# A two-layer decoder step on one core: four changed orders, the last rows by products with diagonals, and 32 gate pages on SP's queue

## What is computed

```python
for i in range(2):
    mk, mv = memory tokens @ w_mem_kv[i]
    # layer 0: indexer-selected sparse attention, layer 1: forgetting attention
    q, k, v, ... = h @ w_in
    so = attend(q, [cache, k], [cache, v])          # layer 1 adds cumulative log-forget bias:
    #   lf_all = concat([pool_lf[page_table], logf_new]); c = cumsum(lf_all)
    mo = mem_attend(qm, mk, mv)
    h = layer_norm(alpha * h + concat(so, mo) @ w_o, ln1_g, ln1_b)
    h = layer_norm(alpha * h + hier_moe(h), ln2_g, ln2_b)   # top-1 of 4 groups, top-2 of 4 experts
return h (prompt rows, sample rows), keys, values, gates
```

## Time and profile before

| | |
|---|---|
| median of 3 runs | 2313.71 us (2310.28 to 2316.61) |
| profiled execution | 2314.92 us, its span 2313.1 us |
| TensorE busy | 2181.2 us, 94% of the span |
| VectorE, ScalarE busy | 669.1 us (29%), 494.5 us (21%) |
| mean granted TensorE clock | 0.973 |
| memory traffic | 647.30 MB, 280 GB/s over the span |

### The profile page before, as it was taken

How to read it: one execution, slowest core, us unless ns; L and a number is a source line. 1 busy time by engine, 2 the same in 40 slices (tenths; PEclk the granted TensorE clock), 3 DMA queues, 4 the chain that set the end, 5 groups by cost and what they waited for, 6 DMA issues and landing times.

```text
span 2313.1 us, 32005 instructions
## 1 busy us (share of the span) xinstructions
PE 2181.2 (94%) x12445; PEld 1369.2 (59%) x12445; DVE 669.1 (29%) x1226; ACT 494.5 (21%) x1115; POOL 4.3 (0%) x10
## 2 busy tenths in 40 slices
PE   8999999989999999999799999999999999998996
PEld 7778875678744344343478886545787343434433
DVE  0249941601652222212400010023017512222224
ACT  1221026400421001011300206633004210100114
POOL 0000000000000000000000000000000000000000
PEclk9999999989899999999899999989898999999998
DMA  9733658784269999999754457998542799999992
GB/s 265 224 146 110 215 159 260 236 291 146 74 262 427 391 429 402 429 392 428 291 170 136 181 174 265 359 323 303 182 146 74 311 416 395 429 393 428 387 426 120
DMA packets 209036, 647.30 MB, mean 280 GB/s; under 512 B 54840, under 2 KB 88393, under 8 KB 183305
## 3 DMA queue, kind: packets, MB, share of 16 engines
q1 hardware_dynamic: 175841, 636.25, 71.4%
q10 hardware_dynamic: 33072, 9.38, 1.9%
HBM read 639.61 MB, written 5.96 MB: 279 GB/s over the span
## 4 chain that ended last, share of the span: by engine, by line
PE 74%; DMA 14%; SPq 5%; DVE 2%; issue 2%; ACTq 1%; ACT 1%; DVEq 0%
PE bank L642 20%; PE bank L1296 13%; PE bank L1135 9%; DMA ring<-in_w_down 8%; PE bank L1326 7%; PE bank L1340 5%; DMA ring<-in_w_up 4%; PE bank L1281 4%; SPq L398 3%; PE bank L876 3%; PE bank L1016 1%; PE bank L886 1%; ACTq L398 1%; PE bank L1188 1%; PE bank L768 1%
## 5 line engine op out<-in xcount | busy, mean ns | idle before, releaser
L1296 PE MATMUL bank<-ring,AT 128*64 128x512 f32 x2048 | 452.1, 599 | 25.1 <-DMA ring<-in_w_up 23.3
L1421 ACT ACTIVATE arena<-bank 128x512 f32<-128x512 f32 (+5 forms) x531 | 262.2, 541 | 877.8 <-PE bank L642 264.0
L642 PE MATMUL bank<-X,ring 128*128 128x264 f32 x1664 | 387.3, 390 | 11.9 <-ACT X L1671 7.3
L642 PEld LDWEIGHTS bank<-X,ring 128*128 128x128 f32 x1664 | 312.9, 191 | 71.1 <-issue 14.5
L1296 PEld LDWEIGHTS bank<-ring,AT 128*64 128x64 f32 x2048 | 147.0, 138 | 320.6 <-issue 286.9
L1326 PE MATMUL bank<-ring,arena 128*64 128x512 f32 x1024 | 233.7, 612 | 44.0 <-DMA ring<-in_w_down 38.7
L1135 PE MATMUL bank<-AT,ring 128*128 128x264 f32 x1024 | 238.2, 396 | 7.1 <-DVEq L2027 7.1
L1135 PEld LDWEIGHTS bank<-AT,ring 128*128 128x128 f32 x1024 | 200.0, 196 | 43.3 <-issue 7.9
L2303 DVE TENSOR_TENSOR X<-bank,X 128x264 f32<-128x264 f32 x256 | 110.8, 433 | 327.9 <-PE bank L1340 325.0
L1326 PEld LDWEIGHTS bank<-ring,arena 128*64 128x64 f32 x1024 | 78.6, 141 | 188.8 <-issue 176.1
L1340 PE MATMUL bank<-arena 128*128 128x264 f32 x512 | 118.2, 389 | 0.0
(11 more groups left out here) (322 smaller groups left out, 1404.8 us busy)
## 6 DMA issues: line engine op xcount, KB each, us to landing
ring<-in_w_gate SPq DMA_DIRECT2D x64, 2048.0 KB, 17.2
ring<-in_w_up SPq DMA_DIRECT2D x64, 2048.0 KB, 13.2
ring<-in_w_down SPq DMA_DIRECT2D x64, 2048.0 KB, 16.3
ring<-in_w_o SPq DMA_DIRECT2D x16, 2048.0 KB, 11.3
ring<-in_cache_b_k SPq DMA_DIRECT2D x128, 256.0 KB, 4.2
ring<-in_cache_b_v SPq DMA_DIRECT2D x128, 256.0 KB, 4.8
ring<-in_w_in_a SPq DMA_DIRECT2D x14, 2048.0 KB, 15.2
ring<-in_w_in_b SPq DMA_DIRECT2D x12, 2048.0 KB, 10.7
```

Of the source, the lines that this page charges most:

```text
L642: mm = pe.matmul(B[4 * (g % 2) + f][:, 0:n_tok], u[:, c * 512 + f * P:c * 512 + (f + 1) * P], src[8 * half + c][:, 0:n_tok], start=(half = ...
L1296: mm = pe.matmul(B[bank][64 * s:64 * s + 64, :], M.xsT[:, at:at + 64], ring[slots[s][0]][:, c * FE:(c + 1) * FE], start=(half == 0 and c = ...
L1421: return act.activation(out, in_, ACT.Copy, scale=scale)
```

## The change

It has six parts. *Gate rows*: in layer 1 TensorE makes them at step 12 in place of 7, and ScalarE copies them ahead of its second group of pages. *Pages*: the 32 pages of sequences 6 and 7 are issued by SP right behind unit q5. *Folds*: a second tile (`a.S[:, 0:512]`, free by then) for the copies, and `ov_copy(x)` waits for fold x-2. *`router_weights`* stands at the start of `mix` on VectorE. *Logits*: the last unit's products stay together, mean of squares and logits follow. *Last rows*: gain and transposition are one product of a raw chunk with a diagonal matrix of the gains (`M.dg`, made by ScalarE during the last quad); mean and bias come in as a product over two rows (`M.fix` with `M.gain`, loaded by SP), and the division by the deviation is the scale of the copy out of the bank, shared by ScalarE and VectorE. The sample rows are stored by SP in four parts.

```diff
+            a.ov = [a.ovs, a.S[:, 0:512]]
...
+        M.rows = [ar(D * t, D) for t in range(2)] + [ar(2 * D, 512)]
+        M.dg = [ar(2 * D + 512 + P * c, P) for c in range(KC)]
...
                         wload(layer, s, win, k % 2, c0 + 512 * (k // 2), 512)
+                        if (layer, name, k) == (1, "q", 5):
+                            sp.wait_ge(S("zeroed"), ZERO_LF)
+                            for b in (6, 7):
+                                pages(S("lf_in"), b, 0, PAGES, i["cache_b_lf"][0],
+                                      lambda g: lay[1].LF[:, g * P + score_row(b):g * P + score_row(b) + H])
...
             def gate_rows(a, x):
 
-                if x == 7:
+                if x == 12:
...
-                            if k == 3 and half == 1 and f == 2:
-                                pe.wait_ge(S("ln_square_used"), 16 * layer + 12)
-                                pe.matmul(B[1][:, 0:T], cst("mean"), M.sqs, start=True, stop=False)
-                                raw_logits(layer, range(8))
...
-                raw_logits(layer, range(8, 12))
-                squares(layer, range(12, KC))
+                pe.wait_ge(S("ln_square_used"), 16 * layer + 12)
+                pe.matmul(B[1][:, 0:T], cst("mean"), M.sqs, start=True, stop=False)
+                raw_logits(layer, range(6))
                 pe.wait_ge(S("rows_summed"), 2 * layer + 2)
                 pe.matmul(B[3][:, 0:T], cst("mean"), M.rstd, start=True, stop=True).then_inc(S("ln_shift"), 1)
-                raw_logits(layer, range(12, KC)).then_inc(S("raw_logits"), 1)
+                squares(layer, range(12, KC))
+                raw_logits(layer, range(6, KC)).then_inc(S("raw_logits"), 1)
...
+            def last_raw(bank, q, t):
+
+                for c in range(4):
+                    pe.matmul(bank[:, c * P:(c + 1) * P], Xc[4 * q + c][:, t * P:(t + 1) * P], M.dg[4 * q + c],
+                              start=(c == 0), stop=False)
+
+            def last_fix(bank, q, t):
+
+                pe.matmul(bank[:, :], M.fix[32 * q:32 * q + 2, t * P:(t + 1) * P], M.gain[32 * q:32 * q + 2, :],
+                          start=False, stop=True).then_inc(S("last_rows"), 1)
...
                     act.wait_ge(S("ov_ready"), 12 * layer + x + 1)
-                    if x:
-                        act.wait_ge(S("ov_turned"), 12 * layer + x)
+                    if x >= 2:
+                        act.wait_ge(S("ov_turned"), 12 * layer + x - 1)
                     w = a.W if x < NB else 512
-                    copy(a.ovs[:, 0:w], B[6 + x % 2][:, 0:w]).then_inc(S("ov_copied"), 1)
+                    copy(a.ov[x % 2][:, 0:w], B[6 + x % 2][:, 0:w]).then_inc(S("ov_copied"), 1)
...
+            def last_rows():
+
+                def row(q, t, n, bank):
+                    act.wait_ge(S("last_rows"), n)
+                    out = M.rows[t][:, 512 * q:512 * (q + 1)]
+                    act.activation(out, bank[:, :], ACT.Copy, scale=M.c1[8][:, t:t + 1]).then_inc(S("token_rows_copied"), 1)
+
+                act.wait_ge(S("row_scale"), 3)
+                row(1, 0, 2, B[3])
+                row(0, 2, 5, B[0])
+                row(0, 1, 6, B[1])
...
                 for k in range(3):
+                    if layer == 1 and k == 1:
+                        gate_rows(a)
                     if layer == 1:
                         load_lf(range(2 * k, 2 * k + 2))
-                    if layer == 1 and k == 1:
-                        gate_rows(a)
                     slab(layer, "q", k, heads(a.qT[:, k * 4 * T:(k + 1) * 4 * T], 4), T, SCALE)
                 if layer == 1:
-                    load_lf(range(6, NB))
...
             def mix(layer):
                 k_ln = 2 * layer
+                router_weights(layer)
...
-                    if k == 0:
-                        router_weights(layer)
```

More of the change, by code:

```diff
@@ L562, in _ @@
                         quad_loads(it, experts)
+            sp.wait_ge(S("low_made"), 2 * N_ITEMS)
+            for k, w in enumerate(("ln2_g", "ln2_b")):
+                sp.dma_start(M.gain[k:P:32, :], i[w][1].rearrange("(q f) -> q f", q=4)).then_inc(S("gain_rows"), 16)
+            sp.wait_ge(S("token_rows_copied"), 2)
+            for q in range(4):
+                sp.dma_start(o["y_sample"].rearrange("b a d -> (b a) d")[:, 512 * q:512 * q + 512],
+                             M.rows[2][32 * q:32 * q + NB, :]).then_inc(S("stored"), 16)
             sp.wait_ge(S("stored"), 16 * N_STORES)
@@ L1405, in _ @@
                 n_quad = experts(layer)
-                layer_norm(layer, n_quad)
-            last_rows()
+                if layer == 0:
+                    layer_norm(layer, n_quad)
+            last_norm(n_quad)
         stores = [0]
@@ L1683, in layer_norm @@
                 act.activation(M.rstd, M.rstd, ACT.Sqrt, bias=cst("eps")).then_inc(S("ln_std"), 1)
-                load_table(ACT.Exp)
-                affine(k)
-            def token_rows():
-                for t in range(3):
-                    rows = P if t < 2 else NB
-                    for q in range(4):
-                        n = 4 * t + q + 1
-                        act.wait_ge(S("last_rows"), n)
-                        copy(M.xtok[0:rows, t * D + 512 * q:t * D + 512 * (q + 1)], B[2 + n % 4][0:rows, :])\
-                            .then_inc(S("token_rows_copied"), 1)
-                    act.wait_ge(S("token_rows_copied"), 4 * t + 4)
-                    dst = o["y_prompt"][0, t * P:(t + 1) * P, :] if t < 2 else o["y_sample"].rearrange("b a d -> (b a) d")
-                    store(dst, M.xtok[0:rows, t * D:(t + 1) * D])
+                if layer == 0:
+                    load_table(ACT.Exp)
+                    affine(k)
+            def last_rows():
[7 more added lines that the diff above has]
+                row(0, 1, 6, B[1])
+                act.wait_ge(S("token_rows_copied"), 3)
+                act.wait_ge(S("ln_normed"), 48 + 3)
+                store(o["y_prompt"][0, 0:P, :], M.rows[0])
+                row(2, 1, 8, B[2])
+                act.wait_ge(S("token_rows_copied"), 4)
+                act.wait_ge(S("ln_normed"), 48 + 5)
+                store(o["y_prompt"][0, P:SEQ, :], M.rows[1])
             def row_high(layer, n):
@@ L1775, in quad @@
                         copy(M.sh, B[7][:, 0:T]).then_inc(S("ln_part_copied"), 1)
+                    if final_quad and layer == 1:
+                        for c in range(KC):
+                            copy(M.dg[c], ident, lnp[:, 80 + c:81 + c]).then_inc(S("ln_scaled"), 1)
                     if not final_quad:
@@ L2378, in _ @@
                 experts(layer)
-                layer_norm(2 * layer + 1)
-        assert stores[0] == N_STORES, stores[0]
+                if layer == 0:
+                    layer_norm(1)
+            last_norm()
+        assert stores[0] + 4 == N_STORES, stores[0]
 QI_AT = H * P + 2 * 256
-N_STORES = 2 + 4 + 2 + 2 + 4 + 2 + 3
+N_STORES = 2 + 4 + 2 + 2 + 4 + 2 + 2 + 4
 LINKS_PER_QUAD = 12
```

78 lines of the change are left out of this document (62 added, 16 removed).

## The result

The changed kernel takes **2283.64 us** (median of 4 runs, 2282.77 to 2284.75), the kernel before 2311.99 us beside it (4 runs, 2306.24 to 2316.61). The ratio is 0.9879, 95% interval 0.9855 to 0.9903: 28 us less (22 to 34). The forecast was 2283 us, range 2275 to 2297. The profiled execution took 2284.26 us, its span is 30.7 us shorter than that of before.

The account below looks back on a forecast made before the run. TensorE is busy nearly throughout; winnable are its waits and half-clock stretches outside the DMA-bound experts. 5.3 + 8.6 + 12.8 + 2.2 + 2.0 = 30.9 us off 2314.9 gives 2284, or 2283 in the median's frame; range 2275 to 2297.

Parts of the forecast that it names:

- The hinge: Expert phases: the weight stream starts when TensorE arrives, so a microsecond saved ahead moves the phase as a whole.
- The experts absorb it: Rival: the weight stream already runs on its own, so only some 4 us show, 2310; chance 0.04.
- (a): Layer 1's query slabs: TensorE's waits of 1.51 and 3.77 us for ScalarE go with gate rows and pages moved, 5.3 us.
- the rule: Trainium skill on pages: a second issuing engine saves only sequencer time, so the edit gives nothing, sum 5.3 us smaller.
- the rival on the pages: Pages gain nothing on SP since something else there is late: 25.6 us in all, 2288; chance 0.04.
- (b): Last folds of each attention: waits for ScalarE's copies shrink, 4.6 and 4.0 us, together 8.6 (5.8 to 11.5).
- if the closer packing keeps it up: Folds and first output matmuls: the clock stays up, and another 1.6 and 1.9 us come back.
- the least case: Folds, low end 5.8 us: the clock falls at the same places and layer 0 keeps only 2.9 us.
- (c): `mix`, both layers: waits for VectorE 7.15 us plus clock behind them, 12.8 together; logits order another 2.2 us.
- waits go, clock does not come back: Rival: only the waits are saved, clock stays low; gains 19.3 us, 2294; chance 0.2.
- (d): Final normalisation after the last expert: 4.6 us less at full clock, 1.2 later at half clock; taken as 2.0 us.
- the least of its likeliest case: Whole kernel: the likeliest case, chance 0.69, spans 2276 to 2291, its least gain given as 23 us.

Follow-up runs that it names:

- experiment 4: Kernel before with only the gate rows moved, all pages staying on ScalarE: ratio 0.9963 to the kernel before, gain 8.6 us.
- experiment 8: Changed kernel with the 32 pages of sequences 6 and 7 back on ScalarE: 2282.65 us, ratio 0.9861 to the kernel before.
- Experiment 3: Kernel before with four unused dense products filling the gap ahead of the wait for `sums_read`, `router_weights` not moved: ratio 0.9986, gain 3.2 us.
- experiment 6: Kernel before with only the logits order changed (last output products together, mean of squares and logits behind): ratio 0.9997, gain 0.7 us.
- experiment 9: Changed kernel run again without edit, on the chip of the next three runs: 2284.77 us, ratio 0.9862 to the kernel before.
- experiment 7: Changed kernel with the old end (normalisation, affine copies and transposes of the last layer as before): 2286.63 us, ratio 0.9876 to the kernel before.
- experiment 10: Changed kernel with the four corrections of the second 128 prompt rows issued together behind all their raw rows: 2277.57 us, ratio 0.9833 to the kernel before.
- experiment 11: Changed kernel with raw rows and corrections of the end in alternation, no product added or removed: 2277.65 us, ratio 0.9836 to the kernel before.
- experiment 12: Changed kernel with four unused dense products between the corrections of the first prompt rows and of the sample rows: 2282.86 us, ratio 0.9862 to the kernel before.

## Why the prediction was right

- **The hinge**, that time saved ahead of the experts moves them as a whole, held. From the gate products to the last sums the fourteen traces take 479.9 to 485.8 us in layer 0 and 479.5 to 485.6 in layer 1, whichever parts they have; before is at 482.4 and 482.6. "The experts absorb it" is out. The 3.1 us of layer 1 are this spread, not a gain: the second trace of before has 3.0 of them, and the changed kernel itself has 479.5 and 485.1.
- **(a), 5.3.** 5.5 in the trace, but not by the two means that I gave equal room: experiment 4 has all of it and experiment 8 shows nothing for the pages. So two prices of the prediction were wrong though the sum was right: the pages do gain nothing on SP, and yet the time is not the 5.3 us longer that the rule and the rival on the pages each took off for that. The waits hung on the order of the gate rows alone. The size was read from one trace; a half clock behind the 3.6 to 3.8 us wait, present in three of the six traces that have this wait, adds 1.7 to 2.6. What the Trainium skill says (DMA: Bandwidth & Descriptors, "Issuing engines are not separate DMA queues"), that a second issuing engine saves only sequencer time, agrees with experiment 8. But sequencer time was not small here, 0.6 us a page: nothing waited for it once the gate rows had moved.
- **(b), 8.6.** Too high: 6.7 in the trace, 3.4 and 3.3. The waits went as counted: up to the router's transposes 7.6 us are gone, 8.0 were forecast. The step that was off is "if the closer packing keeps it up": the clock falls in the folds all the same, only later, and the output products behind them take 0.8 and 0.2 us longer in place of the 1.6 and 1.9 us that full clock would have brought. Of the 2.8 us that I had put on the clock above the least case, 0.9 came.
- **(c), 12.8 and 2.2.** 13.1 in the trace, 14.1 alone. Experiment 3 separates the two halves: 7.2 of waiting, 5.7 of clock. The rival "waits go, clock does not come back" is out here, but comes near to (b). The logits gained 2.8 in place of 2.2 up to the raw rows, and 1.6 more per layer behind them, most of it through the clock, a gain that I had not seen and that the time of experiment 6 does not confirm.
- **(d), 2.0.** 0.5 in the first trace, 2.3 in experiments 8 and 9; the whole time of experiment 7 can't confirm either. The value between the two clocks was fair; where in the tail the clock halves decides 1.1 of the 1.8 us between them. Two things were missed. Corrections are not costed by number: one, two or four in a row take about as long. And the end that has products in place of transposes did not hold the clock: it halved at 2266.9 us, behind single columns and two-row corrections, with TensorE listed as busy without a break from 2252 us on. The Trainium skill (TensorE: Matmul & The Clock Gate, "Part 4: PE-mode transpose") says that transposes do not count as busy for the clock. This did not decide the tail, since the clock fell without them.
- The start of the program (2.8 us) is variation: the changed kernel's second trace has fold 8 at 463.6 us, the first trace of before has it at 464.6. The attention of layer 1 differs by the clock, in two places. From the values to the memory it takes 94.4 to 97.7 us at clocks of 0.93 to 0.90 with no relation to the parts; here before and after are alike (94.4 and 94.5). The 1.6 us lie ahead of the values: every kernel waits 2.29 us there for ScalarE, and behind this wait, from 1488.6 us on, the changed kernel's clock is at 0.50 for 3.4 us. From the turning of the memory to the values it takes 242.1 to 242.2 us in both traces of the changed kernel and in experiments 10 to 12, 240.6 in the first trace of before and in six others (experiments 7 and 8 among them), 243.4 in two. So two executions of the kernel before differ by more (2.7 us), but whether the 1.6 us come with the change is not shown.

That the total came out at 2284 is partly luck: (b) was 1.9 and (d) 1.4 too high, the logits some 4 too low, and the start and the experts' spread cancel. The 23 us that the prediction names as the least of its likeliest case are not its own sum either: its least terms add up to 24.2.

The fastest kernels here are those of experiments 10 and 11: medians of 2277.6 and 2277.7 us, 7 below the changed kernel in the same set, with intervals that still overlap its own. The tails in the traces bear out 2.0 to 3.7 of these 7 for experiment 10 and 0.6 to 2.4 for experiment 11; where the rest comes from is not shown.

## What to carry to other kernels

Price a wait of TensorE together with what the clock does behind it, and test the clock's part alone by filling the gap and keeping the wait; here it was 5.7 of 13.1 us in the traces. When two edits aim at one stall, run each alone: the reordering had everything, the move to another queue nothing. Thin products over a few rows are better issued in one run than one by one, as soon as their inputs exist.

## What the runs showed of the hardware

- One correction (two matmuls over 2 rows with 512 columns) took 1.12 us, two 1.13 and four, on rows 0, 32, 64 and 96, 1.14 us at full clock; at half clock one took 2.07 and two 2.08.
- An unused product of 128x128 by 128x512 in f32 cost 0.9 us (3.60 and 3.70 for four).
- The clock halved behind single columns and two-row corrections although the trace lists TensorE as 100% busy. In one trace each, 3.7 us of dense products among them kept it at 1.00 to the end (experiment 12), and 1.2 us of raw rows in the same place did not (experiment 11).
- The clock of single stretches differs between executions: behind the same wait of 3.6 to 3.8 us it stayed at 1.00 in three traces and stood at 0.50 for a while in three, 1.7 to 2.6 us, and the two traces of the kernel before are one of each. From raw row to gather that kernel has 0.75 in one trace and 0.80 in the other, 1.1 us.
